# Sixteen of eighty half modulation units in the fourth attention's steps, and all half units issued from the weights' queue

## What is computed

```python
c_act = jax.nn.silu(c)                                   # c: (1, 2048)
mod = c_act @ ada_w[l] + ada_b[l]                        # ada_w: (2048, 12288)
sh1, sc1, g1, sh2, sc2, g2 = jnp.split(mod, 6, axis=-1)  # six rows of 2048
h = rmsnorm(x, norm1_g[l]) * (1.0 + sc1[:, None]) + sh1[:, None]
x = x + g1[:, None] * token_mixer(h, ...)   # four attentions of 8 heads, a norm each, @ w_out
h = rmsnorm(x, norm2_g[l]) * (1.0 + sc2[:, None]) + sh2[:, None]
x = x + g2[:, None] * moe_ffn(h, ...)
```

## Time and profile before

| | |
|---|---|
| median of 3 runs | 3036.61 us (3032.55 to 3037.06) |
| profiled execution | 3050.54 us, its span 3048.8 us |
| PE / DVE / ACT busy | 91% / 62% / 42% of the span |
| DMA | 644.87 MB, mean 212 GB/s |
| PE's granted clock, mean | 0.95 |

### The profile page before, as it was taken

The page is one execution under the profiler, slowest core; times in us unless marked ns, Lnnn a source line. Parts: engine busy times, 40 slices in busy tenths (PEclk is TensorE's granted clock), DMA queues, the critical chain, the costliest instruction groups (busy, mean ns, idle before and its releaser), DMA issues.

```text
span 3048.8 us, 36653 instructions
## 1 busy us (share of the span) xinstructions
PE 2775.6 (91%) x14444; PEld 2312.1 (76%) x14444; DVE 1879.5 (62%) x2345; ACT 1274.7 (42%) x1539; POOL 66.9 (2%) x126
## 2 busy tenths in 40 slices
PE   3679989898899999999979898999899999999997
PEld 1267878676788877777679476999787888888886
DVE  6985655556667788888866544444546454445444
ACT  2033433333344467777543133534334443444443
POOL 0011111000000000000000000000000000000000
PEclk9789998799799999999989997999999999999999
DMA  8777765331477789999734242445355655555553
GB/s 322 309 294 255 257 220 202 131 111 60 152 251 259 255 307 363 360 367 365 272 124 179 107 149 110 165 180 182 148 187 172 192 186 193 191 191 193 191 191 116
DMA packets 178526, 644.87 MB, mean 212 GB/s; under 512 B 10923, under 2 KB 10988, under 8 KB 134104
## 3 DMA queue, kind: packets, MB, share of 16 engines
q1 hardware_dynamic: 158688, 551.58, 50.8%
q0 software_dynamic: 16864, 72.88, 6.9%
q10 hardware_dynamic: 2840, 18.56, 1.7%
HBM read 635.59 MB, written 7.39 MB: 211 GB/s over the span
## 4 chain that ended last, share of the span: by engine, by line
PE 64%; DVE 15%; DMA 13%; ACT 4%; issue 3%; DVEq 0%; ACTq 0%; SPq 0%
PE ps L1546 63%; DMA raw<-in_stream 8%; DMA under_r<-in_stream 4%; DVE w_lo L899 3%; ACT w_hi L567 2%; DVE raw L978 2%; DVE under_r L990 2%; DVE arena L958 0%; ACT arena L682 0%; DVE arena L1052 0%; DVE arena L1068 0%; ACT arena L588 0%; DVE arena L960 0%; DVE arena L1451 0%; DVE h_lo L950 0%
## 5 line engine op out<-in xcount | busy, mean ns | idle before, releaser
L899 DVE TENSOR_TENSOR w_lo<-raw,w_hi 128x1024 fp32r<-128x1024 f32 x968 | 1170.9, 1223 | 806.5 <-ACT w_hi L567 803.3
L567 ACT ACTIVATE w_hi<-raw 128x1024 fp32r<-128x1024 f32 x968 | 1010.4, 1057 | 963.2 <-PE ps L1546 861.0
L1546 PE MATMUL ps<-w_hi,h_hi 128*128 128x512 f32 x1216 | 477.3, 393 | 17.7 <-DVE h_lo L1505 10.0
L1546 PE MATMUL ps<-w_hi,r_hi 128*128 128x512 f32 x1184 | 470.3, 397 | 18.2 <-DVE w_lo L899 10.5
L1546 PE MATMUL ps<-w_lo,h_hi 128*128 128x512 f32 x1216 | 475.2, 391 | 0.0
L1546 PE MATMUL ps<-w_hi,h_lo 128*128 128x512 f32 x1216 | 475.0, 391 | 0.0
L1546 PE MATMUL ps<-w_lo,r_hi 128*128 128x512 f32 x1184 | 463.4, 391 | 0.0
L1546 PE MATMUL ps<-w_hi,r_lo 128*128 128x512 f32 x1184 | 463.0, 391 | 0.0
L1546 PE MATMUL ps<-h_hi,w_hi 128*128 128x256 f32 x1536 | 446.8, 291 | 17.8 <-DVE w_lo L899 10.3
L1546 PE MATMUL ps<-h_lo,w_hi 128*128 128x256 f32 x1536 | 442.7, 288 | 0.0
L1546 PE MATMUL ps<-h_hi,w_lo 128*128 128x256 f32 x1536 | 442.0, 288 | 0.0
(11 more groups left out here) (269 smaller groups left out, 1945.9 us busy)
## 6 DMA issues: line engine op xcount, KB each, us to landing
raw<-in_stream SPq DMA_DIRECT2D x524, 1024.0 KB, 5.5
under_r<-in_stream POOLq DMA_DIRECT2D x80, 512.0 KB, 5.6
arena<-in_mod_units ACTq DMA_DIRECT2D x16, 1024.0 KB, 4.9
filters<-arena POOLq DMA_DIRECT2D x4, 1280.0 KB, 5.2
arena<-filters POOLq DMA_DIRECT2D x4, 1280.0 KB, 6.1
x<-in_x POOLq DMA_DIRECT2D x1, 2048.0 KB, 19.1
arena<-bias_rows POOLq DMA_DIRECT2D x2, 1024.0 KB, 10.3
x<-bias_rows POOLq DMA_DIRECT2D x2, 1024.0 KB, 11.2
```

What stands on the lines that cost most here:

```text
L567: act.activation(dst, src, ACT.Copy).then_inc(hi_ready, 1)
L899: dve.tensor_tensor(low, src, high, ALU.subtract).then_inc(lo_ready, 1)
L1546: return pe.matmul(o, a, b, start=start, stop=stop)
```

## The change

- `ASIDE` has one half in two of three steps outside the attentions (before: three of four, and none at four steps near the tables) and one in each step of the first three attentions (before: 13 in 8 steps). By phase, before and now: steps 0 to 23: 15 and 16; first attention 13 and 8; 32 to 47: 12 and 10; second 13 and 8; `small` without step 71: 12 and 10; behind it 2 and 4; third 13 and 8. That makes 80 and 64.
- The other 16 are reduced in the 16 steps of the fourth attention, one at the end of each.
- For them `c_row` has to leave `under_r[:, 0]`, since mixB's norm writes there: ACT copies it to `x[:, 1, :]` (free then) before the exponential of the compressed branch. The slots of these 16 are the last 1024 columns of `under_r[:, 0]` and `under_r[:, 1]`. The load of `x[:, 1, :]` waits for the last half.
- SP issues all half units, between the weights and in DVE's order. POOL's list then has no half units: the two tables of the start come directly one after the other, ahead of the small load of `sinks`; after the second attention the third table comes, then the compression's weights.
- DVE waits before the fourth attention for 48 blocks of `mod` only, and for all 80 before the second norm's gain.

```diff
@@ aside_table
-        if 24 <= k < 32 or 48 <= k < 56 or 72 <= k < 80:
-            counts.append(1 if k % 3 == 1 else 2)
-        else:
-            counts.append(0 if k % 4 == 3 or k in TOEPLITZ_AT else 1)
-    counts[GAP_AT] += ASIDE_HALVES - sum(counts)
+        beside = 24 <= k < 32 or 48 <= k < 56 or 72 <= k < 80
+        counts.append(1 if beside or k % 3 < 2 else 0)
+    counts[GAP_AT] += ASIDE_HALVES - FOURTH_HALVES - sum(counts)
@@ SP
-            for n in range(SLOTS, BASE["moe"]):
-                weight(n)
+            def aside(j):
+                if j >= ASIDE_HALVES:
+                    return
+                if j >= 2:
+                    sp.wait_ge(sem("aside_done"), j - 1)
+                if j == ASIDE_HALVES - FOURTH_HALVES:
+                    sp.wait_ge(sem("c_moved"), 1)
+                sp.dma_start(aside_place(j)[0], sp_units[FIRST_UNITS + j // 2][:, j % 2 * HALF:(j % 2 + 1) * HALF])\
+                    .then_inc(sem(f"aside_landed{j % 2}"), 16)
+            aside(0)
+            aside(1)
+            weight(4)
+            used = 0
+            for k in range(len(ASIDE)):
+                if k % 2 == 0:
+                    weight(k // 2 + 5)
+                for _ in range(ASIDE[k]):
+                    aside(used + 2)
+                    used += 1
+            for t in range(16):
+                for k in share(t):
+                    if k % 2 == 0 and len(ASIDE) // 2 + k // 2 + 5 < BASE["moe"]:
+                        weight(len(ASIDE) // 2 + k // 2 + 5)
+                if t < FOURTH_HALVES:
+                    aside(used + 2)
+                    used += 1
@@ ACT
             norm_root("mixB", ("att_out", 48), 512, mix, mix_junk)
+            act.wait_ge(sem("aside_done"), ASIDE_HALVES - FOURTH_HALVES)
+            copy(c_fourth, c_row).then_inc(sem("c_moved"), 1)
             act.wait_ge(sem("cmp_max"), 1)
             act.activation(cp[:, :, :, 0:N_CMP], cs[:, :, :, 0:N_CMP], ACT.Exp).then_inc(sem("cmp_exp"), 1)
+            act.wait_ge(sem("c_moved"), 1)
@@ DVE, scores
+                    if partial and t < FOURTH_HALVES:
+                        aside_half(ASIDE_HALVES - FOURTH_HALVES + t)
@@ POOL
+            pool.wait_ge(sem("aside_done"), ASIDE_HALVES)
             load("ld_x", (x[:, 1, :], x_rows[:, 1, :]))
```

More of the change, by code:

```diff
@@ L61 @@
 GAP_AT = 71
-TOEPLITZ_AT = (7, 8, 13, 14)
+FOURTH_HALVES = 16
 def aside_table():
@@ L300, in two_blocks, with aside_place @@
         c_row = under_r[:, 0, D:2 * D]
-        aside_slot = under_r[:, 1, D:2 * D].rearrange("p (s n) -> p s n", s=2)
+        c_fourth = x[:, 1, :]
+        def aside_place(j):
+            half = slice(j % 2 * HALF, (j % 2 + 1) * HALF)
+            if j < ASIDE_HALVES - FOURTH_HALVES:
+                return under_r[:, 1, D + j % 2 * HALF:D + (j % 2 + 1) * HALF], c_row[:, half]
+            return under_r[:, j % 2, D + HALF:2 * D], c_fourth[:, half]
         w4 = under_h[0:64, 0, :].rearrange("p (b n) -> p b n", b=4)
@@ L493, in _ @@
                 pool.dma_start(kf_dram[b], ko[b % 2].rearrange("p a n -> p (a n)")).then_inc(sem(f"kf_stored{b % 2}"), 16)
[L496 to L507, removed]
             pool.wait_ge(sem("brow_stored"), 16)
@@ L515, in toeplitz @@
                 load("ld_toep" if m in (0, 3) else "ld_toep2", (toep, src))
+            toeplitz(0, toep)
+            toeplitz(2, toep2)
             load("ld_sink", (stat[:, 32:40], d["sinks"].partition_broadcast(P)))
[L518 to L522, removed]
             pool.wait_ge(sem("att_out"), 16 * 2)
+            toeplitz(1, toep2)
             load("ld_cmp", (w1k, d["w1k"]), (w1v, d["w1v"]), (w2c, d["w2kv"]), (peT, d["pe"]))
-            aside(issued(56), issued(62))
-            toeplitz(1, toep2)
-            aside(issued(62), issued(74))
             pool.wait_ge(sem("cmp_hidden"), 2)
             toeplitz(3, toep)
-            aside(issued(74), ASIDE_HALVES)
-            pool.wait_ge(sem("att_out"), 16 * 3)
+            pool.wait_ge(sem("aside_done"), ASIDE_HALVES)
             load("ld_x", (x[:, 1, :], x_rows[:, 1, :]))
@@ L987, in aside, with aside_half @@
                 for j in range(sum(ASIDE[:k]), sum(ASIDE[:k + 1])):
[L988 to L997, removed]
+                    aside_half(j)
+            def aside_half(j):
+                u, (slot, c) = FIRST_UNITS + j // 2, aside_place(j)
+                if j == ASIDE_HALVES - FOURTH_HALVES:
+                    dve.wait_ge(sem("c_moved"), 1)
+                dve.wait_ge(sem(f"aside_landed{j % 2}"), 16 * (j // 2) + 16)
+                dve.tensor_tensor_reduce(slot, slot, c, 1.0, 0.0, ALU.mult, ALU.add, aside_sums[:, j % 8:j % 8 + 1])\
+                    .then_inc(sem("aside_done"), 1)
+                if j % 8 == 7:
+                    dve.wait_ge(sem("aside_done"), j + 1)
+                    ch(dve.tensor_tensor(mod_sums, aside_sums[:, 0:8:2], aside_sums[:, 1:8:2], ALU.add))
+                    dve.tensor_tensor(mod[:, u - 3:u + 1], mod_sums, col("ada_b", 96)[:, u - 3:u + 1], ALU.add)\
+                        .then_inc(mod_ready, 1)
+                    dve.wait_ge(mod_ready, u // 4 + 1)
             def late_modulation(i):
@@ L1210, in nsa_out @@
                                              ALU.mult, ALU.add).then_inc(sem("att_out"), 1)
-            dve.wait_ge(mod_ready, ADA_UNITS // 4)
+            dve.wait_ge(mod_ready, 3 * DC // 4)
             scores(24, 16, False, nsa_out, partial=True)
@@ L1263, in add_cols @@
                 return step
+            dve.wait_ge(mod_ready, ADA_UNITS // 4)
             gated_norm_gain(4, "norm2")
```

## The result

The changed kernel takes 2999.91 us (median of 4 runs, 2996.80 to 3001.63) against 3036.84 us (3032.55 to 3038.80) of the kernel before. The ratio is 0.9876 with an interval of 0.9864 to 0.9888, so 36.9 us were gained where 26 were forecast. It is the time that the second rival ("more than that") gave.

The account below looks back on a forecast made before the run. PE was taken to bound the kernel, waiting for DVE, which halves delayed. Gains of 14 + 5 + 9 = 28 less 2 lost gave 26 us off the 3036.6 median: 3010.6 us, range 3000 to 3026.

Parts of the forecast that it names:

- more than that: Whole kernel: all 25.5 us of waits go and 12 of the clock's, less 1, giving 3000 us; chance 0.12.
- DVE's lists in the attentions: First three attentions: fewer halves let DVE keep up, taking 14 of PE's 17.4 us of waits for exponentials.
- The text's own check: Three attentions at PE's pace: 50.5 us each instead of 59.3, 26 us for the three alone.
- They were mostly hidden: DVE's 63.4 us of waits for halves, 195 to 503 us: shrink to a few, but mostly cost nothing.
- The compression's weights: In `small`: POOL's loads no longer before a half in its queue, 5 of 8.1 us of `w_lo` waits gained.
- agrees only in part: Trace against the skill's rule of shared engines: the 8.21 us wait in `small` was an order within one queue.
- The clock: Granted clock rises once the pauses are gone: 9 of 20 us gained, bounds 0 and 15.
- The start: First projections: two tables issued together at 196 us slow everything some 25 us; loss of 1.5 us.
- The row of c: Compressed branch: ACT's copy before the exponential costs 0.3 us, uncovered 1.9.
- the fourth attention: Sixteen halves there are covered by DVE's waits for PE: cost 0.2 us, 18 if the cover were gone.
- Slower by a shared queue: Plain phases: weights and halves in one queue make halves land late, 12 us slower, 3049 us; chance 0.06.
- About half: Attentions: DVE's 5.9 and PE's 5.94 us tie, small waits return in each step, 3023 us; chance 0.25.

Follow-up runs that it names:

- twice_in_steps: The changed kernel with the half reduced a second time in five of eight steps of the first three attentions, no second transfer; 3019.91 us, ratio 0.9933.
- oldplain_sp: The changed kernel with the old spacing outside the attentions (three of four steps, none near the tables, one half behind `small`), SP's queue; 3018.28 us, ratio 0.9927.
- before_again: The kernel before, unedited, profiled a second time; 3040.8 us.
- change_again: The changed kernel, unedited, run once more with its own runs of before; 2999.96 us, ratio 0.9870.
- newtable_pool: The changed kernel with the halves issued by POOL again, at the old places in its list; 3008.22 us, ratio 0.9902.
- oldtable_sp: The kernel before with its table of 80 halves, all issued by SP, and POOL's list as in the change; 3038.74 us, ratio 1.0004.
- without16: The changed kernel without the fourth attention's 16 halves (transfers, DVE's work, copy of the row of c); 2999.63 us, ratio 0.9882.

## Why the prediction missed by 11 us

**DVE's lists in the attentions: right in kind, the term too small.** The text took 14 of 17.4 us, leaving the ends of the attentions and the third one's longer steps. All of the row went. `twice_in_steps` brings 12.0 us of waits for exponentials back with DVE work alone. The text's own check ("8 x 5.94 + 3 = 50.5 us", 26 us for the three attentions) was nearer than the sum: the three lost 29.1 us, and two of them took 47.7, that is 8 x 5.96 with nothing left over at the end. The check was higher than the sum's 23 (14 and the clock's 9, part of which was for `small`), and I used it to call the sum cautious, where it should have moved the number.

**"They were mostly hidden": the step that failed.** The late halves outside the attentions had no term, but for 5 us at the compression's weights. `oldplain_sp` puts their spacing and count at 18.4 us with SP's queue, 15 by the ratios. The price shows at two places. The projections took 76.1 us (clock 0.96, PE idle for 4.8) there and 71.8 (0.98, 2.2) in the change, and `small` 84.3 (0.84, 13.5) and 74.5 (0.89, 6.2). PE's waits for `w_lo` between 186 and 605 us are 13.9 us in 4 places there and 3.7 in one in the change. c_k and c_v, which got no term at all, gave 4.3 us against `before_again`, but only 0.7 against `oldplain_sp`; no run says what gave the rest.

The text had the right quantity, the time from issue to use, did not price it, and had its sizes wrong. It worked out 4.4 us with the old spacing and 7.2 with the new one and set them against a median landing. In the traces outside the attentions the shortest times are 3.1 to 3.4 us (`before_again`, `oldplain_sp`) and 4.5 (the change; two behind `small` have 1.1 and 3.8), and the halves that cost are those under way beside POOL's loads, which land well above the median of 6.4 to 7.8 us. From the traces, in us:

| place and run | issue to use | landing | DVE waits | PE waits |
|---|---|---|---|---|
| projections, `oldplain_sp` | 3.4 | 11.0 | 7.6 | 2.6 |
| projections, the change | 4.6 | 10.2 | 5.6 | 0 |
| projections, `change_again` | 4.6 | 11.6 | 7.0 | 0.3 |
| `small`, `oldplain_sp` | 3.4 | 13.6 | 10.2 | 7.3 |
| `small`, the change | 5.8 | 10.8 | 5.0 | 0 |

A half that was 5.6 us late cost PE nothing in these rows; one that was 7.6 or 10.2 us late did. The new spacing brought the late halves to the safe side of that: it added 1.2 and 2.4 us before the use, and the landings were 0.8 and 2.8 us shorter as well. No run changed one of the two alone.

The traces put the queue's 8 us at something else, the place directly behind a table in POOL's list. The old table had no half at the four steps near the tables: in `before_again` the first half behind the second table was issued 6.9 us after it and landed in 9.5. The new table has no such pause. With POOL's queue (`newtable_pool`) a half then stood directly behind the table, landed in 13.9 us, and the projections took 76.7 us. SP's list has no tables; there they took 71.8. No run put the pauses back into the new table, so this reading rests on the landings alone. In the projections of the change:

```profile
raw<-in_stream SPq DMA_DIRECT2D x13, 1024.0 KB, 7.2
under_r<-in_stream SPq DMA_DIRECT2D x16, 512.0 KB, 6.4
arena<-bias_rows POOLq DMA_DIRECT2D x1, 1024.0 KB, 6.6
x<-bias_rows POOLq DMA_DIRECT2D x1, 1024.0 KB, 12.4
```

**The compression's weights: the place right, the cause half wrong.** 5 of 8.1 us were expected from taking POOL's loads out of the way. `oldtable_sp` and `oldplain_sp` took them out and kept the stall (PE 7.26 us in `oldplain_sp`), so the order in the queue, which the text made of the 8.21 us, is not needed for it: in these two runs the half is as slow in another queue, beside the same loads. With the spacing DVE's wait is halved (5.0 us) and PE's is gone. The text set the rule that several issuing engines share the same 16 DMA engines (the Trainium skill, *Trainium Kernel Development and Optimization*, Key Constraints) against a trace that "agrees only in part". With the old spacing the runs agree with the rule: the queue changed the time by 0.04%, and the half in SP's queue took 13.6 us beside POOL's loads. With the new one they do not: 8.3 us, where halves in POOL's queue stood directly behind a table.

**The clock: 9 expected, 15.5 of busy time came, 12.9 by the text's own way of reckoning.** It is the largest error in microseconds beside the spacing. The upper bound of 15 was about reached. More idle time went than was forecast, with the idle time of the late halves too, so that part of this error follows from the other two. In the change the granted clock is 1.00 in the first two attentions. It fell to 0.93 in the third, behind a stretch with 6.2 us of idle time, as the text said it would.

**The start: a loss of 1.5 expected, none came, thanks to the spacing.** The projections took 71.8 us against 72.2. The two tables landed in 6.6 and 12.4 us, before in 11.0 and 12.7. With the old spacing the loss is there: 76.1 us in `oldtable_sp` and `oldplain_sp`, 3 to 4 us more than before, where a half issued at 198.4 us beside the two tables (`oldtable_sp`) took 11.0 us. In the change the loss stayed out because of the spacing, which had no price in the text, so this term came out well by luck.

**The row of c, and the fourth attention: right.** ACT in the compressed branch of the change (answers to the earlier trace rows), then DVE's step that the exponential had waited for:

```profile
537.15 1.90 ACT L600 ACTIVATE x<-under_r 128x2048 f32<-128x2048 f32 x1
539.07 1.28 ACT L755 ACT_TABLE_LOAD   x1
540.36 0.40 ACT L755 ACTIVATE arena<-arena 128x240 f32<-128x240 f32 x1
...
539.59 0.41 DVE L1205 TENSOR_TENSOR arena<-arena,stat 128x240 f32<-128x240 f32 x1
```

DVE is done at 540.00 and the exponential starts 0.36 us later; 0.3 was the forecast. The fourth attention cost -0.5 us against `before_again`, forecast 0.2; `without16` confirms it at 0.3 us by medians.

**The rivals.** *Slower by a shared queue* is false for the change, but with the old spacing its mechanism is there: in the shared queue single halves let DVE wait 9.7 us (`oldtable_sp`) and 10.2 us (`oldplain_sp`), though the median landing is only 5.9 and 6.7 us in the projections. Both halves were under way beside POOL's loads, so that the weights ahead of them in the queue are not shown to be the reason. *About half* lost to *more than that*. The latter's terms (25.5 us of waits, 12 of clock, 1 lost: 36.5) come close to what was measured, 24.6 and 15.5 in stretches that a profile overstates by 4. It had a chance of 0.12 against 0.25, because, as I read it, the text counted every small wait that might return and none of the costs that it had called hidden.

## What to carry to other kernels

Where an engine works through a list in order, compare the length of its step with that of the engine which waits for it, and price the step that is over: here 15 instructions of 1.22 us in steps of 6.7 to 8.8 us cost 17 to 20 us, and 16 of the same kind in steps with slack cost nothing measurable. A prefetch is judged by the time from issue to use against the time to land at the place where most else is under way (here 10 to 14 us, where the median was 6 to 8), and then by what stands ahead of it in its queue. If an independent check of a sum comes out higher than the sum for the same stretches, the number should move towards it, and idle time of PE should be charged with the clock that it costs as well.

## What the runs showed of the hardware

With 24.6 us of pauses gone, PE's busy time for the same products fell by a further 15.5 us, of which the granted clock accounts for 12.9. A transfer of half a megabyte took a median of 6.4 us in the projections of the change, and 10.8 us (the change) to 13.6 us (`oldplain_sp`) beside 3.2 MB that another engine had issued a few us earlier. And a stretch with PE fully busy does not always take the same time. The first attention of the change, once more, in the other profile of the same kernel:

```profile
263.20:312.40 49.20, 49.20 (x331) 42.95 (x332) 29.01 (x69) 21.25 (x57) 0.00 (x0) 0.97 0.51 185
```

It took 49.2 us at a clock of 0.97 against 47.7 at 1.00, with no idle time in either. Of the first and second attentions in all profiles, 13 have no idle time: five took 47.6 to 47.7 us at a clock of 1.00, eight 49.1 to 49.3 us at 0.96 to 0.97, and nothing between. What PE did before the stretch differs little between the two profiles of the change, and no run settles what made the difference; 1.5 us per attention is what comparisons of single profiles are worth here.
